# Depthwise convolution: two of three channel blocks on TensorE in four column tiles, with shifted copies fetched by way of HBM

## The chip, the cores and the metric

The kernel runs on one core of a Trainium2 chip. The metric is the device time of one execution in microseconds (us), the median of several runs. Engines are named as the profile names them: PE is TensorE (PEld its weight loads), DVE is VectorE, ACT is ScalarE, POOL is GpSimd, and SP is SyncE, which here only issues weight loads.

## The reference, cut to what matters

The reference is a stack of three transformer blocks on 256 positions of width 1024, all in fp32: one block with attention and a gated MLP, then two layers that mix the sequence and end in an MLP (dense in the first layer, a mixture of eight experts in the second). Each of the two layers has, among its mixers, a convolution module over 384 channels:

```
h = val * jax.nn.sigmoid(gate)
h = lax.conv_general_dilated(h, w_dw[:, None, :], window_strides=(1,), padding=((30, 0),),
                             feature_group_count=384) + b_dw      # 31 taps, each channel by itself
h = jax.nn.silu(layer_norm(h, ln_g, ln_b))
return h @ w_pw + b_pw
```

The depthwise convolution is 31 multiply-adds for each of 384 x 256 outputs: out[c, t] is the sum over k of w[k, c] * h[c, t - 30 + k]. The layer norm after it runs over the channels.

## The kernel before, in words

Activations of the convolution lie with channels on partitions: `hc[128, 3, 288]` holds three blocks u = 0, 1, 2 of 128 channels, with 32 zero columns ahead of the 256 positions, and `co[128, 3, 256]` takes the convolved blocks.

All weights come as slabs of 1 MB or less, in an order fixed in `plan`. SP loads a slab into a ring of buffers. ACT rounds it to its high part (`splitH`, L1461), DVE subtracts to get the low part (`splitL`, L2159), and PE multiplies three times (high by high, high by low, low by high: L567, L568, L569). ACT and DVE run some slabs ahead of PE (`hi_to`, `lo_to`, `take`). Each engine runs its own instruction stream in program order, and semaphores tie the streams together.

The convolution is inside `mixers(l)`, which is run for the layers l = 0 and 1. The slabs there are, in order: mc (three, for value and gate of blocks 1, 2, 0), mv, mv, mu, mu, ma, mo0, mo1, mo2, mo3.

- DVE's `glu` writes a finished block into `hc` (L2636), in the order 1, 2, 0.
- Blocks 1 and 2 are convolved on DVE, one instruction of 128 x 256 for each tap (L2612 for tap 0, L2615 for the others, which add to `co`). The generator `taps()` gives first three taps of block 1 and then taps of the two blocks in turn, so that two instructions after each other mostly add to different blocks. Each tap waits for the tap before it of its own block. `some_taps(n)` puts n of them between the slab splits: 3, 5, 6, 5, 5, 5, 5, 6, 9 and the 13 that are left. Of these 62, 49 lie ahead of the `catL` writes.
- Block 0 is convolved on PE: for each of the 31 taps one fp32 matmul with a diagonal 128 x 128 matrix as weights and a shifted window of `hc` as moving operand (L1027). The profile shows each fp32 matmul as two passes. POOL builds the 31 diagonal matrices (`diag`, L3119) beforehand, and then zeroes a corner of `wsT`.
- In PE's order these matmuls stand after the pooling mixer (L1005 and L1007, two column tiles of 64), and the spatial gating (L1018), and ahead of the five `cat` units: two by L1037, then three transposes of `yg` (L596). The third transpose uses the bank of the first `cat` unit again and so waits until DVE has written `catL` of that unit (L2169 in DVE's order, after nine taps).
- ACT takes block 0 out of PSUM (L1878), then writes `catH`. After `cat` come the slabs mo0 to mo3 (L567 to L569), with the layer norm's sums between them: L1061 needs all three blocks of `co`.

`catH` and `catL` lie in the buffers RBH and RBL, and so did `diag`.

Of the kernel before, what the change touches and what calls it, by code (L numbers as in the profile page):

```python
# [14 lines left out]
CAP = 128  # L15
# [27 lines left out]
def shape_constants(cap):  # L43
# [43 lines left out]
    "in_x0 in_x1 in_cb in_prm0 in_half in_rope in_prm in_mem in_mask in_grow in_band in_layer in_rt "  # L87
    "out_main out_over zero dwdiag "
# [63 lines left out]
def program(nc, x, mem, consts, w, out, cap):  # L152
    ctx = ExitStack()
    with ctx:
# [21 lines left out]
        diag = at("diag", [128, 31, 128], b0 + 64 * KB)  # L176
# [10 lines left out]
        ph = b0 + 4 * KB  # L187
        ident, ones = cb[:, 0:128], cb[:, 128:256]
# [50 lines left out]
        hc = at("hc", [128, 3, 288], ph + 35 * KB)  # L239
# [314 lines left out]
        def tensor(e):  # L554
# [406 lines left out]
            def mixers(l):  # L961
# [25 lines left out]
                t.wait_ge(S.in_layer, 80 * (l + 1))  # L987
# [10 lines left out]
                for m in range(2):  # L998
                    b = bank["pool", l, m] = ring.take()
                    t.wait_ge(S.mrow, 6 * l + 6)  # L1000
                    t.wait_ge(S.in_band, 16)
# [9 lines left out]
                for tb in range(2):  # L1011
                    b = bank["gm", l, tb] = ring.take()
                    t.wait_ge(S.ws, 2 * l + 2)
                    t.wait_ge(S.dwdiag, 32 * l + 32)
# [7 lines left out]
                b = bank["dw", l] = ring.take()  # L1022
                t.wait_ge(S.dwdiag, 32 * l + 31)
                t.wait_ge(S.th, 3 * l + 3)
                o = claim(b, (S.co0, l + 1))
                for k in range(31):
                    mm = e.matmul(o[:, 0:256], diag[:, k, :], hc[:, 0, 2 + k:258 + k], start=(k == 0), stop=(k == 30))  # L1027
                mm.then_inc(S.dw, 1)

                ring.go(range(4, 8))  # L1030
                for m in range(2):
                    b = bank["cat", l, m] = ring.take()
                    t.wait_ge(S.py, 2 * l + m + 1)
                    t.wait_ge(S.in_layer, 80 * (l + 1))
# [16 lines left out]
                for tb in range(2):  # L1051
# [3 lines left out]
                    if tb == 0:  # L1055
                        b = bank["colsum", l] = ring.take()
                        t.wait_ge(S.taps, 62 * (l + 1))
                        t.wait_ge(S.co0, l + 1)
# [392 lines left out]
        def scalar(e):  # L1451
# [287 lines left out]
            def ffn(f):  # L1739
# [42 lines left out]
                for i in range(12):  # L1782
                    G, V = fb[i % 2], fb[2 + i % 2]
                    if i == 3:
                        if f == 0:
# [3 lines left out]
                            load(band[:, :, :].rearrange("p g t -> p (g t)"), consts[:, c0:c0 + width], S.in_band)  # L1789
                            layer_loads(0)  # L1790
                        else:
# [3 lines left out]
                            a.wait_ge(S.in_grow, 16)  # L1795
# [31 lines left out]
            def mixers(l):  # L1827
# [7 lines left out]

                hi_to(mc[0] + 1)
# [297 lines left out]
        def vector(e):  # L2134
# [274 lines left out]
            def gained(i):  # L2409
                tb, o = i // 2, slice(512 * (i % 2), 512 * (i % 2) + 512)  # L2410
                v.wait_ge(S.xadd, 12)
                v.wait_ge(S.in_grow, 16)
                e.tensor_tensor(xg[:, tb, o], X[:, tb, o], grow[:, o], ALU.mult).then_inc(S.gx, 1)
# [181 lines left out]
            def mixers(l):  # L2595
# [3 lines left out]
                tapped = [62 * l]  # L2599

                def taps():

                    at = {}
                    order = [(k, 1) for k in range(3)]
                    order += [(k - 3 * (u == 2), u) for k in range(3, 34) for u in (1, 2)]
                    for k, u in order:
                        if k < 31:
                            o, src = co[:, u, :], hc[:, u, 2 + k:258 + k]
                            wk = prm[:, dwc + u + 3 * k:dwc + u + 3 * k + 1]
                            if k == 0:  # L2610
                                v.wait_ge(S.th, 3 * l + u)
                                ins = e.tensor_scalar(o, src, wk, pcol("conv_dw_b_2", 3 * l + u), ALU.mult, ALU.add)  # L2612
                            else:
                                v.wait_ge(S.taps, at[u])
                                ins = e.scalar_tensor_tensor(o, src, wk, o, ALU.mult, ALU.add)  # L2615
                            ins.then_inc(S.taps, 1)
                            tapped[0] += 1
                            at[u] = tapped[0]
                            yield
# [650 lines left out]
```

## Time and profile before

| what | value |
|---|---|
| median of 3 runs | 1807.03 us (1806.54 to 1807.79) |
| the profiled execution, its own time | 1805.34 us |
| its span in the profile | 1803.5 us |
| mean granted PE clock | 0.998 of 2.4 GHz |
| PE busy | 1734.2 us, 96% of the span |
| DVE busy | 1183.6 us, 66% |
| ACT busy | 913.9 us, 51% |
| POOL busy | 55.9 us, 3% |

The profile is of one execution, which took 1.7 us less than the median; 1.8 us of that execution's time lie outside the span. The convolution of layer 0 lies between 513 and 571 us, that of layer 1 between 796 and 854 us. The shares of busy time are averages over the whole program. What a change in one stretch is worth has to be read from that stretch.

### The profile page before, as it was taken

Reading aid. Unit: us, or ns where it says so; the run is one execution under the profiler, and the core shown is the slowest. Engines: PE = TensorE matmul, PEld = TensorE weight load, DVE = VectorE, ACT = ScalarE, POOL = GpSimd, SP = SyncE. Lnnn points to the kernel's source line nnn. Section 1 sums busy time; section 2 is a strip of 40 time slices with the busy share of each in tenths; the row PEclk is TensorE's granted clock in tenths of the full one; section 3 lists DMA queues with packets and bytes.
Section 4 is the critical chain, followed back from the end, with each engine's and each line's share of the span. In section 5 each row is a group of like instructions: output and inputs, shape, how many; then the busy total and the mean of one; then the engine's idle time right before and its main releaser. Section 6 shows DMA issues by size and latency. Waiting matters only on the chain.

```text
span 1803.5 us, 25131 instructions
## 1 busy us (share of the span) xinstructions
PE 1734.2 (96%) x10391; PEld 1421.9 (79%) x10391; DVE 1183.6 (66%) x1517; ACT 913.9 (51%) x992; POOL 55.9 (3%) x71
## 2 busy tenths in 40 slices
PE   7999998999999999999999999999999999999997
PEld 7988887899897999998777777776776777676774
DVE  6664576866788665579677665665665665765653
ACT  5445655554464444344556553555455555454542
POOL 0000000000060000050000000000000000000000
PEclk9999999999999999999999999999999999999999
DMA  9433443565544465645659999999999999999995
GB/s 322 157 94 122 151 148 113 176 233 187 170 158 140 138 219 176 209 125 203 233 210 360 370 402 383 418 412 400 364 386 383 404 385 409 410 386 400 404 410 210
DMA packets 157545, 495.13 MB, mean 275 GB/s; under 512 B 9609, under 2 KB 99439, under 8 KB 114415
## 3 DMA queue, kind: packets, MB, share of 16 engines
q1 hardware_dynamic: 152911, 489.04, 71.6%
q10 hardware_dynamic: 4512, 4.40, 0.9%
q8 instruction: 84, 1.38, 0.3%
q14 instruction: 38, 0.31, 0.0%
HBM read 492.36 MB, written 1.05 MB: 274 GB/s over the span
## 4 chain that ended last, share of the span: by engine, by line
PE 81%; DVE 11%; ACT 6%; issue 2%; DMA 0%; ACTq 0%; DVEq 0%
PE bank L567 22%; PE bank L569 21%; PE bank L568 21%; DVE splitL L2159 6%; PE bank L1233 4%; PE bank L1266 4%; ACT splitH L1461 4%; PE bank L1212 1%; DVE co L2615 1%; PE bank L1168 1%; PE bank L1027 1%; PE bank L596 1%; PE bank L710 1%; PE bank L733 1%; PE bank L1085 0%
## 5 line engine op out<-in xcount | busy, mean ns | idle before, releaser
L2159 DVE TENSOR_TENSOR splitL<-raw,splitH 128x2048 fp32r<-128x2048 f32 (+1 forms) x248 | 561.5, 2272 | 155.3 <-ACT splitH L1461 154.5
L1461 ACT ACTIVATE splitH<-raw 128x2048 fp32r<-128x2048 f32 (+2 forms) x250 | 469.5, 1889 | 118.5 <-PE bank L569 106.8
L567 PE MATMUL bank<-RAH,splitH 128*128 128x256 f32 x1088 | 311.7, 286 | 7.1 <-DVE RAL L2169 3.3
L569 PE MATMUL bank<-RAH,splitL 128*128 128x256 f32 x1088 | 307.7, 283 | 0.0
L568 PE MATMUL bank<-RAL,splitH 128*128 128x256 f32 x1088 | 307.7, 283 | 0.0
L567 PE MATMUL bank<-splitH,RBH 128*128 128x512 f32 x736 | 293.4, 399 | 3.3 <-DVE splitL L2159 3.3
L569 PE MATMUL bank<-splitH,RBL 128*128 128x512 f32 x736 | 287.5, 391 | 0.0
L568 PE MATMUL bank<-splitL,RBH 128*128 128x512 f32 x736 | 286.9, 390 | 0.0
L2159 DVE TENSOR_TENSOR splitL<-rawx,splitH 128x2048 fp32r<-128x2048 f32 x89 | 203.1, 2288 | 28.6 <-ACT splitH L1461 28.1
L567 PEld LDWEIGHTS bank<-RAH,splitH 128*128 128x128 f32 x1088 | 208.4, 192 | 11.8 <-DVE RAL L2169 4.5
L568 PEld LDWEIGHTS bank<-RAL,splitH 128*128 128x128 f32 x1088 | 208.5, 192 | 1.0
L569 PEld LDWEIGHTS bank<-RAH,splitL 128*128 128x128 f32 x1088 | 208.5, 192 | 0.0
L1461 ACT ACTIVATE splitH<-rawx 128x2048 fp32r<-128x2048 f32 x89 | 169.6, 1913 | 64.8 <-PE bank L569 64.5
L567 PEld LDWEIGHTS bank<-splitH,RBH 128*128 128x128 f32 x736 | 138.5, 188 | 39.5 <-DVE splitL L2159 10.6
L569 PEld LDWEIGHTS bank<-splitH,RBL 128*128 128x128 f32 x736 | 138.2, 188 | 29.9
L568 PEld LDWEIGHTS bank<-splitL,RBH 128*128 128x128 f32 x736 | 138.5, 188 | 26.4
L567 PE MATMUL bank<-splitH,hTH 128*128 128x512 f32 x280 | 112.9, 403 | 24.1 <-DVE splitL L2159 24.1
L1461 ACT ACTIVATE hTH<-bank 128x512 fp32r<-128x512 f32 x35 | 21.0, 599 | 204.7 <-PE bank L1212 204.7
L2877 DVE TENSOR_TENSOR hTL<-bank,hTH 128x512 fp32r<-128x512 f32 x35 | 24.1, 688 | 135.4 <-ACT hTH L1461 135.4
L568 PE MATMUL bank<-splitL,hTH 128*128 128x512 f32 x280 | 109.4, 391 | 0.0
L569 PE MATMUL bank<-splitH,hTL 128*128 128x512 f32 x280 | 109.1, 390 | 0.0
L1233 PE MATMUL bank<-raw,xgS 128*64 128x256 f32 x864 | 100.5, 383 | 0.0
(340 smaller groups left out, 2217.7 us busy)
## 6 DMA issues: line engine op xcount, KB each, us to landing
raw<-in_moe_wg SPq DMA_DIRECT2D x71, 1024.0 KB, 7.5
raw<-in_moe_wd SPq DMA_DIRECT2D x69, 1024.0 KB, 8.7
raw<-in_moe_wu SPq DMA_DIRECT2D x68, 1024.0 KB, 9.0
rawx<-in_moe_wu SPq DMA_DIRECT2D x44, 1024.0 KB, 8.5
rawx<-in_moe_wd SPq DMA_DIRECT2D x43, 1024.0 KB, 9.0
rawx<-in_moe_wg SPq DMA_DIRECT2D x41, 1024.0 KB, 9.4
raw<-in_w_in SPq DMA_DIRECT2D x24, 1024.0 KB, 6.5
raw<-in_w_up SPq DMA_DIRECT2D x22, 1024.0 KB, 5.1
```

Source lines behind the costliest of these rows:

```text
L567: e.matmul(o, lh, rh, start=start, stop=False)
L568: e.matmul(o, lh, rl, start=False, stop=False)
L569: return e.matmul(o, ll, rh, start=False, stop=stop)
L596: mm = e.transpose(o[:, tb * 128:tb * 128 + 128], src[:, tb, k * 128:(k + 1) * 128], ident)
L710: mm = e.matmul(o[c][:, x0:x0 + wide], qA[p0:p0 + 64, h // 2, tb * 128:tb * 128 + 128], kA[p0:p0 + 64, h // 2, 0:wide], start=True, stop=True)
L733: mm = e.matmul(o[(j % 2) * 64:(j % 2) * 64 + 64, tb * 128:tb * 128 + 128], vA[:, sb, h * 64:(h + 1) * 64], PT[q % 2][:, x0 * 128:(x0 + 1) ...
L1027: mm = e.matmul(o[:, 0:256], diag[:, k, :], hc[:, 0, 2 + k:258 + k], start=(k == 0), stop=(k == 30))
L1233: mm = e.matmul(o[64 * h:64 * h + 64, 0:256], xgS[:, kk, 64 * (j - 5):64 * (j - 4)], V[:, k, 256 * h:256 * h + 256], start=kk == 0, stop=k ...
L1266: mm = e.matmul(banks[2][64 * half:64 * half + 64, :], hTS[q % 2][:, 128 * k + 64 * s:128 * k + 64 * s + 64], V[:, k, 512 * half:512 * hal ...
L1461: return e.activation(o, src, ACT.Copy)
L2159: e.tensor_tensor(l[:, 0:size], raws[home[n]][:, 0:size], h[:, 0:size].bitcast(F), ALU.subtract)\
L2877: e.tensor_tensor(hTL[q % 2][:, :], banks[bank["h", q]][:, :], hTH[q % 2][:, :].bitcast(F), ALU.subtract).then_inc(S.ht_lo, 1)
```

## The change

Block 0 and block 2 are now both convolved on PE, and DVE keeps block 1 alone.

For a PE block, four taps are stacked on the 128 rows of the array: partition 32 j + c of a new tile `hs` holds channel c of a group of 32 channels, shifted by j positions. There are four groups of 32 channels (i), each with its own 32 columns of the array, so that its output lands on partitions 32 i to 32 i + 31 of one bank. Eight matmuls (g) cover 32 taps, the last one with zero weights. The weights (`stack`, eight 128 x 32 matrices for each i and each of two blocks, 1 MB for a layer) are laid out on the host and loaded by ACT's queue at the start of `mixers(l)`.

The shifted copies can't be made within a partition, so POOL's queue writes the block from SBUF to HBM and then reads it back four times, each time one position further, into 32 partitions of `hs`. It waits for the write before it issues the reads, and for the reads before it goes on to the next block. Block 2 comes first, then block 0. The diagonal matrices and their building on POOL are gone. The order of `some_taps` calls is as before, but the generator now has 31 taps, each of which waits for the one right before it.

```diff
+        stack = at("stack", [128, 2, 4, 8, 32], b0 + 64 * KB)
+        hs = [at("hs2", [128, 4, 288], b0 + 72 * KB)]
...
+        hs.append(at("hs0", [128, 4, 288], ph + 42 * KB))
...
-                b = bank["dw", l] = ring.take()
-                t.wait_ge(S.dwdiag, 32 * l + 31)
-                t.wait_ge(S.th, 3 * l + 3)
-                o = claim(b, (S.co0, l + 1))
-                for k in range(31):
-                    mm = e.matmul(o[:, 0:256], diag[:, k, :], hc[:, 0, 2 + k:258 + k], start=(k == 0), stop=(k == 30))
-                mm.then_inc(S.dw, 1)
+                t.wait_ge(S.in_layer, 96 * (l + 1))
+                for v in range(2):
+                    b = bank["dw", l, v] = ring.take()
+                    t.wait_ge(S.hs, 160 * l + 80 * v + 80)
+                    o = claim(b, (S.co0, 2 * l + v + 1))
+                    for g in range(8):
+                        for i in range(4):
+                            mm = e.matmul(o[32 * i:32 * i + 32, 0:256], stack[:, v, i, g, :],
+                                          hs[v][:, i, 2 + 4 * g:258 + 4 * g], start=(g == 0), stop=(g == 7))
+                    mm.then_inc(S.dw, 1)
...
+                load(stack[:, :, :, :, :].rearrange("p v i g c -> p (v i g c)"), stacks[l], S.in_layer)
                 hi_to(mc[0] + 1)
...
-                a.wait_ge(S.dw, l + 1)
-                e.activation(co[:, 0, :], banks[bank["dw", l]][:, 0:256], ACT.Identity,
-                             bias=pcol("conv_dw_b_2", 3 * l)).then_inc(S.co0, 1)
+                for v in range(2):
+                    a.wait_ge(S.dw, 2 * l + v + 1)
+                    e.activation(co[:, 2 - 2 * v, :], banks[bank["dw", l, v]][:, 0:256], ACT.Identity,
+                                 bias=pcol("conv_dw_b_2", 3 * l + 2 - 2 * v)).then_inc(S.co0, 1)
...
-                    order = [(k, 1) for k in range(3)]
-                    order += [(k - 3 * (u == 2), u) for k in range(3, 34) for u in (1, 2)]
-                    for k, u in order:
...
+                    o = co[:, 1, :]
+                    for k in range(31):
+                        src = hc[:, 1, 2 + k:258 + k]
+                        wk = prm[:, dwc + 1 + 3 * k:dwc + 1 + 3 * k + 1]
...
+                            v.wait_ge(S.taps, tapped[0])
+                            ins = e.scalar_tensor_tensor(o, src, wk, o, ALU.mult, ALU.add)
...
+            def shifted(l, v, u):
+                g.wait_ge(S.th, 3 * l + v + 2)
+                e.dma_start(turned_out[l, v], hc[:, u, :]).then_inc(S.hs, 16)
+                g.wait_ge(S.hs, 160 * l + 80 * v + 16)
+                for j in range(4):
+                    e.dma_start(hs[v][32 * j:32 * j + 32, :, :],
+                                turned_out[l, v][:, j:j + 288].rearrange("(i c) x -> c i x", i=4)).then_inc(S.hs, 16)
+                g.wait_ge(S.hs, 160 * l + 80 * v + 80)
...
             for l in range(2):
-                dwc = PCOL["conv_dw_w_2"] + 93 * l
-                g.wait_ge(S.xadd, 12 + 8 * l)
-                for k in range(31):
-                    e.tensor_scalar(diag[:, k, :], ident, prm[:, dwc + 3 * k:dwc + 3 * k + 1], None, ALU.mult)\
-                        .then_inc(S.dwdiag, 1)
-                g.wait_ge(S.ws_turn, l + 1)
-                g.wait_ge(S.dwdiag, 32 * l + 31)
-                e.memset(wsT[64:128, :, 0:64], 0.0).then_inc(S.dwdiag, 1)
+                for v, u in enumerate((2, 0)):
+                    shifted(l, v, u)
```

Waits follow from this: PE and DVE wait for six loads of a layer in place of five (`in_layer`), L1061's sums wait for 31 taps and both PE blocks, DVE's `dd` waits for both too, since `hs` of block 0 lies where `dd` is written, and the zeroing of `wsT` is done once, early.

## Rows read from the trace of the kernel before

**Rows 1.** Stretches: busy us of PE, PEld, DVE, ACT, POOL; then PEclk, DMA share, GB/s.

```profile
511.00:562.00 51.00, 49.93 (x323) 46.30 (x322) 48.76 (x111) 26.93 (x40) 18.11 (x19) 1.00 0.58 190
794.00:845.00 51.00, 50.44 (x330) 47.15 (x329) 46.92 (x98) 25.02 (x37) 16.82 (x19) 1.00 0.59 200
```

**Rows 2.** PE's waits from 510 to 570 us: total, times, longest.

```profile
PE bank L596 <- DVE RBL L2169: 0.5, 1, 0.5
PE bank L567 <- DVE splitL L2159: 0.3, 1, 0.3
```

**Rows 3.** PE's timeline in layer 0: start, us, instruction, [idle before <- releaser].

```profile
546.62 13.58 PE L1027 MATMUL bank<-hc,diag 128*128 128x256 f32 x62
560.13 1.08 PE L1037 MATMUL bank<-py,plw 64*64 64x256 f32 x8
...
562.33 0.44 PE L596 MATMUL bank<-cb,yg 128*128 128x128 f32 x2 [0.54 <-DVE RBL L2169]
```

**Rows 4.** PE's timeline in layer 1.

```profile
829.84 13.58 PE L1027 MATMUL bank<-hc,diag 128*128 128x256 f32 x62
843.35 1.08 PE L1037 MATMUL bank<-py,plw 64*64 64x256 f32 x8
```

**Rows 5.** DVE's timeline in layer 0.

```profile
516.39 1.00 DVE L2615 SCALAR_TENSOR_TENSOR co<-hc,prm,co 128x256 f32<-128x256 f32 x2
...
518.68 0.42 DVE L2636 TENSOR_TENSOR hc<-bank,sgc 128x256 f32<-128x256 f32 x1
...
528.36 0.42 DVE L2636 TENSOR_TENSOR hc<-bank,sgc 128x256 f32<-128x256 f32 x1
...
531.92 2.06 DVE L2615 SCALAR_TENSOR_TENSOR co<-hc,prm,co 128x256 f32<-128x256 f32 x5
...
554.24 1.88 DVE L2676 SCALAR_TENSOR_TENSOR yg<-bank,prm,uu 128x96 f32<-128x96 f32 x8
...
558.24 3.64 DVE L2615 SCALAR_TENSOR_TENSOR co<-hc,prm,co 128x256 f32<-128x256 f32 x9
561.80 0.87 DVE L2169 SCALAR_TENSOR_TENSOR RBL<-bank,prm,RBH 128x256 fp32r<-128x256 f32 x2
```

**Rows 6.** DVE's timeline in layer 1.

```profile
801.72 0.42 DVE L2636 TENSOR_TENSOR hc<-bank,sgc 128x256 f32<-128x256 f32 x1
...
840.32 3.65 DVE L2615 SCALAR_TENSOR_TENSOR co<-hc,prm,co 128x256 f32<-128x256 f32 x9
844.56 0.92 DVE L2169 SCALAR_TENSOR_TENSOR RBL<-bank,prm,RBH 128x256 fp32r<-128x256 f32 x2 [0.60 <-ACT RBH L1497]
```

**Rows 7.** Costliest groups, two column tiles of 64, all of the run: busy us, mean ns.

```profile
L1233 PE MATMUL bank<-raw,xgS 128*64 128x256 f32 x864 | 100.5, 383 | 0.0
```

**Rows 8.** PE's timeline in layer 0, two column tiles of 64.

```profile
543.25 0.66 PE L1005 MATMUL bank<-band,at_rows 128*64 128x256 f32 x4 [0.56 <-ACT at_rows L1861]
543.74 0.40 PE L1007 MATMUL bank<-band,at_rows 128*64 128x128 f32 x4
543.95 0.65 PE L1005 MATMUL bank<-band,at_rows 128*64 128x256 f32 x4
```

**Rows 9.** Groups of instructions, 510 to 600 us: passes of two columns.

```profile
L1068 PE MATMUL bank<-cb,sq 128*128 128x2 f32 x12 | 1.5, 253 | 0.2 <-ACT sq L1891 0.2
```

**Rows 10.** DMA issues: count, KB each, median us from issue to landing.

```profile
out<-Z SPq DMA_DIRECT2D x2, 512.0 KB, 3.2
...
c<-in_shape_constants ACTq DMA_DIRECT2D x1, 164.0 KB, 12.0
cb<-in_shape_constants ACTq DMA_DIRECT2D x1, 128.0 KB, 4.3
```

**Rows 11.** Busy time by stretch: mixers' start, and the experts.

```profile
500.00:510.00 10.00, 9.34 (x76) 8.90 (x75) 8.23 (x36) 8.15 (x17) 9.62 (x14) 1.00 0.02 8
...
1000.00:1700.00 700.00, 679.24 (x3538) 493.23 (x3537) 446.61 (x303) 364.73 (x288) 0.00 (x0) 1.00 0.98 395
```

**Rows 12.** PE's waits from 1000 to 1700 us, all of them.

```profile
PE bank L567 <- DVE splitL L2159: 20.8, 18, 1.2
```

More of the change, by code:

```diff
@@ L149, in halves, with program @@
     return (0, 2, 1, 3).index(tb_half) + 1
-def program(nc, x, mem, consts, w, out, cap):
+def program(nc, x, mem, consts, stacks, w, out, cap):
     ctx = ExitStack()
@@ L1056, in mixers @@
                         b = bank["colsum", l] = ring.take()
-                        t.wait_ge(S.taps, 62 * (l + 1))
-                        t.wait_ge(S.co0, l + 1)
+                        t.wait_ge(S.taps, 31 * (l + 1))
+                        t.wait_ge(S.co0, 2 * l + 2)
                         o = claim(b, (S.dd, 6 * l + 3))
@@ L1788, in ffn @@
                             c0, width = CCOL["band"]
-                            load(band[:, :, :].rearrange("p g t -> p (g t)"), consts[:, c0:c0 + width], S.in_band)
+                            load(band[:, :, :].rearrange("p g t -> p (g t)"), consts[:, c0:c0 + width], S.in_grow)
                             layer_loads(0)
@@ L2598, in mixers @@
                 dwc = PCOL["conv_dw_w_2"] + 93 * l
-                tapped = [62 * l]
+                tapped = [31 * l]
                 def taps():
-                    at = {}
-                    order = [(k, 1) for k in range(3)]
-                    order += [(k - 3 * (u == 2), u) for k in range(3, 34) for u in (1, 2)]
-                    for k, u in order:
[L2607 to L2619, printed above, removed]
+                    o = co[:, 1, :]
+                    for k in range(31):
+                        src = hc[:, 1, 2 + k:258 + k]
+                        wk = prm[:, dwc + 1 + 3 * k:dwc + 1 + 3 * k + 1]
+                        if k == 0:
+                            v.wait_ge(S.th, 3 * l + 1)
+                            ins = e.tensor_scalar(o, src, wk, pcol("conv_dw_b_2", 3 * l + 1), ALU.mult, ALU.add)
+                        else:
+                            v.wait_ge(S.taps, tapped[0])
+                            ins = e.scalar_tensor_tensor(o, src, wk, o, ALU.mult, ALU.add)
+                        ins.then_inc(S.taps, 1)
+                        tapped[0] += 1
+                        yield
                 more = taps()
@@ L3250, in by_slabs, with tap_stacks @@
     return np.ascontiguousarray(m.reshape(8, 2, 4, 128, 7, 512).transpose(0, 4, 1, 3, 2, 5)).reshape(8, 7, 2, 128, 2048)
+def tap_stacks(taps):
+    rows = np.zeros((2, 32, 384), np.float32)
+    rows[:, 0:31] = taps
+    rows = rows.reshape(2, 8, 4, 3, 4, 32).transpose(0, 2, 5, 3, 4, 1)[:, :, :, [2, 0]]
+    stacks = np.zeros((2, 4, 32, 2, 4, 8, 32), np.float32)
+    for c in range(32):
+        stacks[:, :, c, :, :, :, c] = rows[:, :, c]
+    return stacks.reshape(2, 128, 2048)
 def kernel(**inputs):
@@ L3266 @@
     out = nc.dram_tensor("out_0", (1, 256, 1024), F, kind="ExternalOutput").ap()
-    program(nc, aps["x"], aps["mem"], aps["shape_constants"], {n: aps[n] for n in WEIGHTS}, out, CAP)
+    program(nc, aps["x"], aps["mem"], aps["shape_constants"], aps["stacks"], {n: aps[n] for n in WEIGHTS}, out, CAP)
     r = run_bass_kernel_spmd(nc, [feeds], core_ids=[0])
```

33 lines of the change are left out of this document (20 added, 13 removed).

## The prediction

> **What bounds the kernel now.** I read the busy time by stretch first. In both stretches of the convolution PE is busy for all but about 1 us of 51, at a granted clock of 1.00, and DVE for all but 2 to 4 us [rows 1]. So neither share alone names the bound: each may be late for the other. PE's waits say who is late: in layer 0 it waits for DVE twice, 0.3 us for a slab's low part and 0.5 us for `catL` [rows 2]. PE is the bound by a hair, and DVE stands right behind it. The timelines then give the place where the two meet in both layers: the third transpose of `yg` (L596), which can't start before DVE has written `catL` of the first `cat` unit. I call its start the meeting point. In layer 0 it is at 562.33, 0.53 us after DVE began that write at 561.80, and PE had waited 0.54 us [rows 3, 5]. In layer 1 DVE was done with its taps at 840.32 + 3.65 = 843.97, waited 0.60 us for ACT and began the write at 844.56 [rows 6], so the meeting point is 844.56 + 0.53 = 845.09. ACT's way from PE's first `cat` matmul to that write is 844.56 - 843.35 = 1.21 us [rows 4, 6]; the way from PE's last convolution matmul to the meeting point is thus 1.21 + 0.53 = 1.74 us when DVE isn't late. Behind it PE runs slabs that were split long before, so what the meeting point gains, the end gains.
>
> **PE's convolution.** Removed: 31 matmuls, 62 passes, 13.58 us in each layer [rows 3, 4], 0.219 us a pass. Added: 2 blocks x 8 x 4 matmuls = 64, 128 passes of as many columns (256). The trace has no four column tiles of 32. It has two of 64: 864 passes took 100.5 us, 0.116 each [rows 7], against 0.219 for the full array, so two tiles run side by side. Bounds: from 128 / 4 x 0.219 = 7.0 us, if four do too, to 128 x 0.116 = 14.9 us, if four do no better than two. Weight loads don't stand against the lower one: passes of two columns, which cost little but their load of 128 columns, took 1.5 / 12 = 0.125 us [rows 9]; a quarter of that, four times, is 0.125 in a period of 0.219. Nor does the rate of instructions, as far as the trace goes: eight passes with their loads started in 543.95 - 543.25 = 0.70 us, 0.088 each [rows 8], which the array itself set; four tiles need 0.055. I take 7.0: what limits two tiles there is the streaming of columns, and each tile has its own.
>
> The Trainium skill's page TensorE: Matmul & The Clock Gate (Part 3, measured speedup) gives 2.38x for three column tiles; at that efficiency four would give 3.2x and the convolution would take 28.0 / 3.2 = 8.8 us, an estimate. The same page's Part 1 has about 62 ns of sequencer time per matmul where hardware decoding is off: 128 of them make 7.9 us. The rows here show neither for four tiles.
>
> **DVE's taps.** Two blocks in turn: nine taps less five take 3.64 - 2.06 = 1.58 us, 0.395 each; the last of five then lasts 2.06 - 4 x 0.395 = 0.48. Two taps of one block, the second waiting for the first, take 1.00, so they start 0.52 apart [rows 5]. The new generator has only such taps. Of the 49 taps ahead of the meeting point the first three stay as they are. The other 46 cost 46 x 0.395 = 18.2 us; the 28 that replace them come in groups of 5, 6, 5, 5, 5, 2, and cost 22 x 0.52 + 6 x 0.395 = 13.8 us. DVE reaches its `catL` write 4.4 us earlier, not the 7.1 that 18 taps fewer would give. All 31 are done before L1061's sums, and the 13 late ones go from a place where PE didn't wait for them: 0.
>
> There is also a loss. The groups of 5 and 6 lie ahead of the last mu slab's split, with 9 starts 0.125 us later each: 1.1 us. In layer 0 PE already waited 0.3 for that split [rows 2], so PE is 1.1 us later from there on, and starts the convolution at 546.62 + 1.1 = 547.7. In layer 1 no such wait is on the list, and I take 0.
>
> The skill's page VectorE: DVE Perf Modes (The DRAIN you can't avoid) says that a semaphore between two instructions costs nothing extra. These rows show 0.125 us for it, and go before the rule; what it would make of the sum is a rival below.
>
> **The sum.** Layer 0: by PE the meeting point comes at 547.7 + 7.0 + 1.74 = 556.4, by DVE at 562.33 - 4.4 = 557.9. The later one holds: 4.4 us. Layer 1: by PE 829.84 + 7.0 + 1.74 = 838.6, by DVE 843.97 - 4.4 + 0.53 = 840.1, against 845.09: 5.0 us. Together 9.4. So DVE becomes the bound at this point, and PE's convolution may take up to 557.9 - 1.74 - 547.7 = 8.5 us in layer 0 and 8.5 in layer 1 at no cost. Above that each us costs one in each layer.
>
> **The transfers.** Block 2 is in `hc` at 518.68 + 0.42 = 519.1, block 0 at 528.8 [rows 5]. PE wants block 2 at 547.7 and block 0 3.5 us later, at 551.2. POOL does one trip after the other: a write of 150 KB, its landing, four reads of about 147 KB, their landing. POOL issues no DMA in this trace. Nearest rows, issue to landing: 3.2 us for a write, 4.3 for 128 KB, 12.0 for 164 KB behind other loads [rows 10]. A trip is between 3.2 + 4.3 = 7.5 and 24 us. I take 10, nearer to the low rows, since the DMA engines are busy 0.58 of the time here [rows 1]; it ends at 529 and 539, long before. PE never waits up to a trip of (551.2 - 519.1) / 2 = 16.0 us, in layer 1 (833.3 - 802.1) / 2 = 15.6 [rows 4, 6]; with DVE's lateness as a further cover the meeting point stays up to (557.9 - 1.74 - 3.5 - 519.1) / 2 = 16.8 and 16.4. Beyond it nobody but PE is held, but behind PE stand the `cat` units and all the rest.
>
> **At nothing.** ACT issues the load of `stack`, 1 MB, as the mixers begin, in a stretch (500 to 510) where the DMA engines are busy 0.02 of the time [rows 11]; PE first asks for the layer's loads behind the last mu slab, which it can't start before DVE's taps at 531.92 [rows 5]. Block 2's way out of PSUM runs on ACT while PE convolves block 0. The diagonal matrices: nobody waited for POOL at the convolution; if POOL slowed DVE, its going gives at most some tenths, and I count 0. From `cat` on, the experts' stage included, the gain is carried on: from 1000 to 1700 the DMA engines are busy 0.98 of the time [rows 11], but PE waits 20.8 us of 700 in all, and none of it for a DMA [rows 12].
>
> The profiled execution took 1805.34 us, 1.8 more than its span; less 9.4 that is 1795.9. The median of the runs stands 1.7 us above it, so 1807.03 - 9.4 = 1797.6. This kernel's runs tell a change from none at about 0.2%, 3.6 us.
>
> **Rivals.**
>
> A. *Three tiles' worth*: the four tiles overlap only in part. At 28.0 / 3 = 9.3 us the cover of 8.5 is passed by 0.8 in each layer: 1799.2; at 11 us, 1802.6. Nothing in the trace speaks for it but that nothing shows more than two.
>
> B. *Pairs only*: 14.9 us. Layer 0: 547.7 + 14.9 + 1.74 = 564.3, 2.0 late; layer 1: 846.5, 1.4 late: 1810.4, no change that can be told. It loses its point if passes of one tile show starts 0.22 apart.
>
> C. *Transfers late*, the one on the other side: the trip is longer than 16.8 us. Each us more comes twice, once for each block, in each layer, 4 us in all: the gain of 9.4 is gone at 18.9 us a trip, and it is slower by over 0.2% from 19.8. At 24: block 0 lands at 567.1, the meeting point is at 567.1 + 3.5 + 1.74 = 572.3, 10.0 late, in layer 1 10.3 late: 1827. For it: a busy queue did take 12.0 a step. Against: that was behind a row of others. The skill's page SBUF - State Buffer (SBUF: two separate sides) adds that POOL builds its DMAs' descriptors itself and is locked out of SBUF while DVE runs in a two-port mode: 3.1 in place of 0.62 us in its example. Two steps of 2.5 us more would still leave the trip of 10 at 15, an estimate; no run here shows it.
>
> D. *Taps cheaper than read*: a tap that waits costs no more than one that doesn't, as by the page on VectorE. DVE gains 7.1 us, and PE sets the meeting point: layer 0 at 546.62 + 7.0 + 1.74 = 555.4, 6.9 earlier, layer 1 6.5 earlier: 1793.6. The row of 1.00 us speaks against it.
>
> E. *Swallowed by the experts' stage*: its loads bound it, and layer 1's 5.0 us are lost: 1802.6.
>
> **Chances.** The forecast 0.59, A 0.12, B 0.09, C 0.11, D 0.06, E 0.03. Faster are the forecast, A, D and E: 0.80. Within 0.2%: B but for its edge and a little of C, 0.09. Slower: the rest, 0.11. The range leaves out B and C, 0.20, and takes in D at the low end and A and E at the high: 1793 to 1805.
>
> **What the new profile would show.** L1027's successor in about 7 us a layer, two blocks of 3.5, the tiles' passes starting in fours; DVE's taps 0.52 apart, its `catL` write at about 557.4 and 839.6; PE waiting about 1.5 us for DVE at the meeting point and 1.4 at the last mu split of layer 0; POOL's trips of about 10 us, ended before PE asks. A wait of PE at the first convolution matmul would show C, passes at 0.11 us B. The prediction is wrong if DVE, now the bound, has a wait in its chain that I took as its own work.

## The result, and the profile after

| | before | after |
|---|---|---|
| median of the runs (four each) | 1806.78 us | 1795.63 us |
| ratio of the two, 95% interval | | 0.9942 (0.9930 to 0.9954) |
| the profiled execution, its span | 1803.5 us | 1794.3 us |
| PE, DVE, ACT, POOL busy | 1734.2, 1183.6, 913.9, 55.9 us | 1723.7, 1160.2, 914.4, 12.5 us |

The ratio is 10.5 us faster (8.3 to 12.6); the medians stand 11.1 apart, the spans 9.2. Forecast were 9.4 us and 1797.6.

The stretches up to the meeting points, columns as in [rows 1]:

```profile
511.00:558.00 47.00, 44.76 (x399) 39.84 (x397) 43.98 (x92) 27.95 (x41) 5.62 (x10) 1.00 0.71 216
785.00:836.00 51.00, 49.42 (x441) 44.95 (x440) 46.14 (x101) 29.07 (x42) 5.48 (x10) 1.00 0.67 206
```

DVE is busy for all but 3 us of 47, though it lost half its taps, and PE has 2.2 us idle where it had 1.1: both have less to do, and neither was left far ahead. PE's waits in layer 0, from 505 to 570 us (total, times, longest), where [rows 2] had 0.5 and 0.3:

```profile
PE bank L599 <- DVE RBL L2177: 1.1, 1, 1.1
PE bank L570 <- DVE splitL L2167: 1.0, 1, 1.0
PE bank L1008 <- ACT at_rows L1868: 0.8, 1, 0.8
```

PE's timeline in both layers (start, us, instruction, [idle before <- releaser]), which answers to [rows 3, 4]. L1032 is the convolution, L599 the transposes, L570 a slab's high by high pass, L1008 the pooling:

```profile
533.82 0.45 PE L570 MATMUL bank<-splitH,RAH 128*128 128x384 f32 x1 [0.98 <-DVE splitL L2167]
...
545.33 0.66 PE L1008 MATMUL bank<-band,at_rows 128*64 128x256 f32 x4 [0.76 <-ACT at_rows L1868]
...
548.79 7.12 PE L1032 MATMUL bank<-hs,stack 128*32 128x256 f32 x128
...
558.58 0.44 PE L599 MATMUL bank<-cb,yg 128*128 128x128 f32 x2 [1.08 <-DVE RBL L2177]
...
826.18 7.12 PE L1032 MATMUL bank<-hs,stack 128*32 128x256 f32 x128
...
835.91 0.44 PE L599 MATMUL bank<-cb,yg 128*128 128x128 f32 x2 [1.02 <-DVE RBL L2177]
```

L1032 takes 7.12 us where the diagonal matrices took 13.58 [rows 3, 4]. The meeting point, the last L599 row of each layer, moved from 562.33 to 558.58 and from 845.09 to 835.91, and PE waits there 1.08 and 1.02 us for DVE. DVE's timeline in layer 0, as [rows 5]:

```profile
516.88 0.41 DVE L2617 TENSOR_SCALAR co<-hc,prm 128x256 f32<-128x256 f32 x1
...
519.94 2.56 DVE L2620 SCALAR_TENSOR_TENSOR co<-hc,prm,co 128x256 f32<-128x256 f32 x5
...
525.76 3.08 DVE L2620 SCALAR_TENSOR_TENSOR co<-hc,prm,co 128x256 f32<-128x256 f32 x6
...
532.01 1.75 DVE L2167 TENSOR_TENSOR splitL<-raw,splitH 128x1536 fp32r<-128x1536 f32 x1
...
550.93 1.00 DVE L2620 SCALAR_TENSOR_TENSOR co<-hc,prm,co 128x256 f32<-128x256 f32 x2
...
555.85 2.28 DVE L2167 TENSOR_TENSOR splitL<-raw,splitH 128x2048 fp32r<-128x2048 f32 x1
558.05 0.87 DVE L2177 SCALAR_TENSOR_TENSOR RBL<-bank,prm,RBH 128x256 fp32r<-128x256 f32 x2
```

Five taps take 2.56 us and six 3.08, each 0.52 more than one less. The split that PE waited for starts at 532.01. Ahead of `catL` (L2177) stands one more split, 2.28 us long, of a slab (mo3) that PE needs much later.

The first tap of this execution is at 516.88, that of before at 515.90, ahead of all of the change's work. Measured from the first tap, the meeting point of layer 0 is 4.7 us earlier (41.70 in place of 46.43) and that of layer 1 5.4 (first taps at 795.17 and 798.93: 40.74 in place of 46.16). So a better measure than the span is the stretch that holds all that the change touches: from the first tap of layer 0 to the layer norm's sums of layer 1 (L1067, 843.02; L1061, 852.23 before). It takes 326.14 us in place of 336.33, 10.2 less, close to the 10.5 of the ratio. Behind it both kernels take 951.3 us.

### The profile page after: what moved, and what is told of

Same layout as the page of the kernel before. It is cut to its first block, busy times and chain, and to the rows that moved or that the text cites. A ratio compares the mean times of both kernels' runs of the same rounds, so it can differ in the third digit from the quotient of the medians.

```text
span 1794.3 us, 25298 instructions
## 1 busy us (share of the span) xinstructions
PE 1723.7 (96%) x10523; PEld 1409.2 (79%) x10523; DVE 1160.2 (65%) x1455; ACT 914.4 (51%) x994; POOL 12.5 (1%) x29
## 4 chain that ended last, share of the span: by engine, by line
PE 79%; DVE 13%; ACT 6%; issue 2%; DMA 0%; ACTq 0%; DVEq 0%
PE bank L570 21%; PE bank L572 21%; PE bank L571 21%; DVE splitL L2167 7%; PE bank L1239 4%; ACT splitH L1467 4%; PE bank L1272 4%; DVE co L2620 2%; PE bank L1218 1%; PE bank L1174 1%; PE bank L599 1%; PE bank L713 1%; PE bank L736 1%; PE bank L1091 0%; DVE fb L2502 0%
## 5 line engine op out<-in xcount | busy, mean ns | idle before, releaser
L570 PE MATMUL bank<-RAH,splitH 128*128 128x256 f32 x1088 | 312.4, 287 | 6.2 <-DVE RAL L2177 3.3
L570 PE MATMUL bank<-splitH,RBH 128*128 128x512 f32 x736 | 293.9, 399 | 3.2 <-DVE splitL L2167 3.2
L570 PEld LDWEIGHTS bank<-RAH,splitH 128*128 128x128 f32 x1088 | 209.4, 192 | 10.6 <-DVE RAL L2177 4.5
L570 PEld LDWEIGHTS bank<-splitH,RBH 128*128 128x128 f32 x736 | 138.7, 189 | 39.5 <-DVE splitL L2167 10.5
L570 PE MATMUL bank<-splitH,hTH 128*128 128x512 f32 x280 | 112.8, 403 | 24.1 <-DVE splitL L2167 24.1
```

What stands on the lines that cost most here:

```text
L570: e.matmul(o, lh, rh, start=start, stop=False)
```

## The experiments

All times are compared with the kernel before on the same chip. A ratio has an interval of some 0.0012 to each side, 2.2 us, so smaller differences rest on the traces. The table has the stretch from the first tap of layer 0 to the sums of layer 1, worked out from each profile as above. Ahead of it and behind it lies the same work in every kernel, and its length scatters: the first tap lies at 515.3 to 517.0 us, the rest takes 951.0 to 951.7 us in nine of the profiles and 952.7 to 953.2 in five, whatever the kernel. The granted clock tells those profiles apart. The four with their first tap at 516.9 us (after, after_again, two_sums, tile_by_tile) have 3.4 us at half clock (1.2 GHz) from about 498 us on, and the five with the longer rest have such a stretch that begins between 874 and 889 us; the others have neither. Just ahead of the one near 498 us PE had waited 1.92 us for DVE, in the kernel before as well, where the clock stayed at 1.00, so what makes it fall in one execution and not in the other stays open. Here is that stretch in the kernel after (columns as in [rows 1]):

```profile
497.80:501.10 3.30, 3.30 (x12) 2.72 (x10) 2.00 (x5) 1.90 (x6) 0.00 (x0) 0.50 0.60 217
```

taps_in_line has such a stretch inside the measured one as well, of which more below.

| kernel | median, us | ratio (95%) | stretch, us | against after |
|---|---|---|---|---|
| before | 1806.78 | | 336.33 | +10.2 |
| after | 1795.63 | 0.9942 (0.9930 to 0.9954) | 326.14 | |
| after_again | 1796.46 | 0.9945 (0.9931 to 0.9959) | 327.07 | +0.9 |
| tiles_alone | 1807.41 | 1.0009 (1.0000 to 1.0018) | 338.13 | +12.0 |
| taps_alone | 1809.15 | 1.0016 (1.0007 to 1.0025) | 338.07 | +11.9 |
| split_late | 1794.26 | 0.9934 (0.9920 to 0.9948) | 324.04 | -2.1 |
| two_sums | 1792.47 | 0.9923 (0.9909 to 0.9937) | 322.63 | -3.5 |
| taps_in_line | 1798.38 | 0.9961 (0.9947 to 0.9975) | 328.23 | +2.1 |
| seven_late | 1791.39 | 0.9924 (0.9910 to 0.9938) | 322.57 | -3.6 |
| block_more | 1801.38 | 0.9974 (0.9963 to 0.9985) | 332.18 | +6.0 |
| tile_by_tile | 1823.99 | 1.0096 (1.0080 to 1.0111) | 354.05 | +27.9 |
| write_twice | 1800.11 | 0.9960 (0.9946 to 0.9973) | 333.51 | +7.4 |
| trip_twice | 1840.21 | 1.0189 (1.0173 to 1.0205) | 370.52 | +44.4 |
| conv_early | 1789.92 | 0.9919 (0.9905 to 0.9933) | 321.59 | -4.5 |

> The kernel after once more, unchanged, beside the three others. All theories: about 11 us under the kernel before, as in its first runs; DVE's taps 0.52 us apart, PE's waits at the meeting points 1.0 to 1.1 us.

It came as expected, but for the wait at layer 0's meeting point, of which more below.

### Each part alone

**tiles_alone**: block 0 in four tiles, DVE with both other blocks.

```diff
-                for v in range(2):
+                for v in (1,):
                     b = bank["dw", l, v] = ring.take()
...
+                    order = [(k, 1) for k in range(3)]
+                    order += [(k - 3 * (u == 2), u) for k in range(3, 34) for u in (1, 2)]
```

> From the kernel after; PE convolves block 0 alone in four column tiles, DVE has the taps of blocks 1 and 2 again, two blocks in turn as before (the load of stack and both trips stay; complete computation). My theory, that PE and DVE were both at their limit at the meeting point: PE's convolution takes 3.56 us in place of 13.58 in each layer, but the catL write still comes where DVE's 49 taps end, as before: nothing gained in layer 0, 0.6 us in layer 1, where DVE no longer waits for ACT. About 0.6 us under the kernel before, no change that can be told, and PE waits some 9 us for DVE at the meeting point. Rival, that PE's shorter convolution alone gave the gain: 2 x 10.0 = 20 us faster, or at least as fast as the kernel after (11 us under before).

Measured: no faster than before, the stretch 1.8 us longer. PE's timeline in layer 0:

```profile
546.26 3.66 PE L1032 MATMUL bank<-hs,stack 128*32 128x256 f32 x64
...
555.74 1.12 PE L599 MATMUL bank<-cb,yg 128*128 128x128 f32 x4 [4.80 <-DVE yg L2684]
561.89 0.69 PE L599 MATMUL bank<-cb,yg 128*128 128x128 f32 x2 [5.04 <-DVE RBL L2177]
```

PE was done with its convolution 10 us sooner and waited all of it away, 4.80 us for `yg` and 5.04 for `catL`. The meeting point is at 561.89, 0.44 earlier. The stretch behind it shows why even that is lost (columns as in [rows 1]):

```profile
561.00:567.00 6.00, 5.11 (x16) 4.16 (x17) 5.86 (x17) 0.38 (x1) 0.00 (x0) 0.63 0.27 94
```

The granted clock is 0.63 on average in these 6 us, after the idle time, and 16 passes of PE fall in them; in the kernel before it is 1.00 from 562 to 568 us, with 26 passes. Layer 1 shows the same: 0.69 from 845 to 851 us, 19 passes for 28. The rival, that the shorter convolution alone gives the gain, falls.

**taps_alone**: the kernel before with DVE's taps of block 1 alone. It leaves out the convolution of block 2, whose place gets the values of block 0.

```diff
                     o = claim(b, (S.co0, 2 * l + 2))
...
-                e.activation(co[:, 0, :], banks[bank["dw", l]][:, 0:256], ACT.Identity,
-                             bias=pcol("conv_dw_b_2", 3 * l)).then_inc(S.co0, 1)
+                for u in (2, 0):
+                    e.activation(co[:, u, :], banks[bank["dw", l]][:, 0:256], ACT.Identity,
+                                 bias=pcol("conv_dw_b_2", 3 * l + u)).then_inc(S.co0, 1)
```

> From the kernel before; DVE has only the 31 taps of block 1, each waiting for the one before it, and PE convolves block 0 with diagonal matrices as before. Block 2 is not convolved: ACT writes PE's block 0 to its place as well. My theory: DVE is 4.4 us earlier at the catL write, but PE's 13.58 us set the meeting point: 0.46 us gained in layer 0, 1.1 lost there by the later mu split, 0 in layer 1: about 0.6 us over the kernel before, no change that can be told. Rival, that DVE's fewer taps alone gave the gain: 8.8 to 11 us faster.

Measured: no faster than before either, the stretch 1.7 us longer. DVE's timeline, then PE's:

```profile
525.33 3.38 DVE L2613 SCALAR_TENSOR_TENSOR co<-hc,prm,co 128x256 f32<-128x256 f32 x6
...
563.23 0.88 DVE L2170 SCALAR_TENSOR_TENSOR RBL<-bank,prm,RBH 128x256 fp32r<-128x256 f32 x2 [5.21 <-ACT RBH L1497]
```

```profile
548.38 13.58 PE L1027 MATMUL bank<-hc,diag 128*128 128x256 f32 x62
...
563.77 0.44 PE L596 MATMUL bank<-cb,yg 128*128 128x128 f32 x2 [0.22 <-DVE RBL L2170]
```

DVE is 5 us ahead at `catL` and waits for ACT, which waits for PE. PE starts its convolution 1.76 us later than before (1.6 measured from the first tap), since the mu split, with dependent taps ahead of it, holds it 1.5 us (0.3 before [rows 2]). So each part alone makes the kernel no faster, and both together take 10.2 us off the stretch: PE and DVE were level, and the meeting point follows the later one.

### Who is the bound at the meeting point now

**split_late**: DVE's split of mo3 moved behind the `catL` writes.

```diff
-                lo_to(n + 4)
                 some_taps(9)
...
                     split_cols(S.cat_lo, catL[:, 2 + u, :], catH[:, 2 + u, :], banks[bank["cat", l, 2 + u]][:, 0:256])
+                lo_to(n + 4)
```

> From the kernel after; DVE's split of the slab mo3 (2.28 us), which stands right ahead of the catL writes, is moved behind them (complete computation). My theory, that DVE is the bound at the meeting point by 1.08 and 1.02 us: both waits of PE go, the meeting point is then PE's last convolution pass plus 1.74 us, 1.0 us earlier in layer 0 and 0.95 in layer 1: 1.9 us under the kernel after. Rival, that the wait comes from ACT's catH and not from DVE's place in its order: no change against the kernel after. Second rival, that mo3's split is then late for PE: slower than after by up to 2.3 us a layer.

Measured: the stretch is 2.1 us shorter than after, for 1.9 expected (the ratio alone couldn't tell). Both rivals fall: the waits at the meeting points are gone, and PE waits nowhere for mo3's split. The three transposes now follow each other:

```profile
555.09 1.17 PE L599 MATMUL bank<-cb,yg 128*128 128x128 f32 x6
```

**two_sums**: odd and even taps add to two sums.

```diff
-                    o = co[:, 1, :]
+                    sums = (co[:, 1, :], sq[:, 2, :])
                     for k in range(31):
+                        o = sums[k % 2]
...
-                            v.wait_ge(S.taps, tapped[0])
+                            v.wait_ge(S.taps, at[k % 2])
...
+                    e.tensor_tensor(sums[0], sums[0], sums[1], ALU.add).then_inc(S.taps, 1)
```

> From the kernel after; DVE's taps of block 1 add in turn to two sums, so that no tap waits for the one right before it; one more instruction adds the two sums (complete computation). My theory, that a tap that waits costs 0.125 us more: taps start 0.395 apart, DVE is 22 x 0.125 = 2.75 us earlier at the catL write and 1.1 at the last mu split. PE's waits of 1.0 us at that split in layer 0 and of 1.08 and 1.02 at the meeting points all but go: 2.95 us under the kernel after. Rival, that the 0.52 us are not the dependence but the price of any tap in this place: no change against after.

Measured: the stretch is 3.5 us shorter, for 2.95. Two taps that follow each other start 0.39 us apart, so the rival falls:

```profile
519.64 0.48 DVE L2624 SCALAR_TENSOR_TENSOR sq<-hc,prm,sq 128x256 f32<-128x256 f32 x1
520.03 0.48 DVE L2624 SCALAR_TENSOR_TENSOR co<-hc,prm,co 128x256 f32<-128x256 f32 x1
```

**taps_in_line**: the same, with the wait for the tap right before.

```diff
-                            v.wait_ge(S.taps, at[k % 2])
+                            v.wait_ge(S.taps, tapped[0])
```

> As two_sums, but each tap still waits, by its semaphore, for the tap right before it, though that one adds to the other sum (complete computation). It tells apart whether 0.52 us between starts comes from reading what the last instruction wrote or from waiting for its end at all. My theory: from the wait; taps start 0.52 us apart as in the kernel after, and the time is that of the kernel after, or 0.5 us a layer over it for the one instruction more. Rival, that a semaphore between two instructions costs nothing by itself: 0.395 us apart, and the time of two_sums, about 3 us under the kernel after.

Measured: the taps are 0.52 apart, and the rival falls. The stretch is 5.6 us longer than that of two_sums, but not all of it is the taps':

```profile
518.86 0.48 DVE L2624 SCALAR_TENSOR_TENSOR co<-hc,prm,co 128x256 f32<-128x256 f32 x1
519.38 0.48 DVE L2624 SCALAR_TENSOR_TENSOR sq<-hc,prm,sq 128x256 f32<-128x256 f32 x1
```

In this execution the clock was at half speed behind the meeting point of layer 0, first here, then the same work in the kernel after:

```profile
558.30:561.70 3.40, 3.40 (x10) 2.63 (x9) 0.49 (x2) 0.02 (x1) 0.00 (x0) 0.50 0.89 297
```

```profile
558.90:562.30 3.40, 3.40 (x18) 2.78 (x17) 1.01 (x4) 0.38 (x1) 0.00 (x0) 1.00 0.87 279
```

Half of 3.4 us is 1.7 us of PE's work. Without it the stretch is about 0.4 us over the kernel after, as expected, and 3.9 over two_sums. Both kernels read and write the same data; only the semaphore that a tap waits for differs. So the 0.125 us are the price of waiting for the end of the instruction right before. PE waits 1.7 and 1.2 us at the meeting points, more than in the kernel after, which has one instruction (0.42 us) less.

**seven_late**: the taps of the kernel after, with seven of them behind `catL`.

```diff
                 glu(1, 2)
-                some_taps(5)
...
                 for n in mu:
                     take(n)
-                    some_taps(5)
+                    some_taps(5 if n == mu[0] else 0)
...
-                some_taps(6)
...
-                some_taps(9)
```

> From the kernel after; the same 31 taps, each waiting for the one before it, but seven of them stand behind the catL writes in place of none: the group of five ahead of the last mu split is left out, and the groups behind it end seven short (complete computation). My theory, that late taps lie where nobody waits for DVE: the wait at the last mu split of layer 0 (1.0 us) goes, DVE reaches the catL writes 3.6 us earlier and both waits at the meeting points go (1.08 and 1.02): about 3 us under the kernel after, as two_sums. Rival, that taps behind catL delay the layer norm's sums or the splits of mo: seven x 0.52 = 3.6 us come back in each layer, and it is up to 4 us slower than the kernel after.

Measured: the stretch is 3.6 us shorter, for 3. DVE's timeline in layer 0:

```profile
553.95 0.92 DVE L2177 SCALAR_TENSOR_TENSOR RBL<-bank,prm,RBH 128x256 fp32r<-128x256 f32 x2
...
555.77 3.60 DVE L2620 SCALAR_TENSOR_TENSOR co<-hc,prm,co 128x256 f32<-128x256 f32 x7
```

The seven taps follow at 555.77, and no wait of PE answers to them. Late taps are free, as the prediction had it.

**block_more**: PE convolves block 0 twice.

```diff
-                    for g in range(8):
...
+                    for again in range(1 + v):
+                        for g in range(8):
...
```

> From the kernel after; PE convolves block 0 twice over into the same bank (128 + 64 passes; the result is the same). This puts a price on PE's time behind the cover: the convolution takes 7.12 + 3.56 = 10.68 us in each layer, of which the 1.08 and 1.02 us that PE waited for DVE are hidden. My theory (what passes the cover costs its full length): 2 x 3.56 - 2.10 = 5.0 us over the kernel after. Rival, that DVE's lateness covers more, or the later stages take it up: less than 2 us over after. Rival, that DVE isn't the bound at all: 7.1 us over.

Measured: 6.0 us longer, for 5.0. The convolution took 10.57 us in each layer, 3.45 more; 2 x 3.45 - 2.10 = 4.8, and in layer 1 PE waited 1.8 us for `at_rows` in place of 0.6, which makes 6.0. Both waits at the meeting points are gone. What passes DVE's cover costs its full length, and both rivals fall.

### The tiles

**tile_by_tile**: the same 128 passes, all of one tile first.

```diff
-                    for g in range(8):
-                        for i in range(4):
+                    for i in range(4):
+                        for g in range(8):
```

> From the kernel after; the same 128 passes for the two blocks, but all eight matmuls of one column tile one after another, then the next tile's, in place of the four tiles in turn (complete computation). My theory, that tiles run side by side only when the passes of different tiles follow each other: passes of one tile start 0.219 us apart, the convolution takes about 128 x 0.219 = 28 us less what neighbouring tiles share, in place of 7.12: about 2 x 21 - 2.1 = 39 us over the kernel after. Rival, that PE looks far enough ahead to overlap them in any order, or that a pass of 32 columns is short in itself: no change.

Measured: 27.9 us longer. PE's timeline, and the passes of L1032 that start in two microseconds (PE busy, PEld busy, clock, DMA share, GB/s), first here, then in the kernel after:

```profile
548.93 21.99 PE L1032 MATMUL bank<-hs,stack 128*32 128x256 f32 x128
```

```profile
549.00:551.00 2.00, 2.00 (x10) 1.04 (x11) 1.00 0.84 342
```

```profile
549.00:551.00 2.00, 2.00 (x44) 1.19 (x40) 1.00 0.85 348
```

Ten passes in 2 us in place of some forty: passes of one tile start 0.22 us apart, as those of the full array do. The whole is 21.99 us and not 28, since the single records show the first passes of the next tile starting while the last three or four of the tile before still run. The loss is 2 x 14.87 - 2.10 = 27.6 us. My 39 had too little overlap in it; the rival falls.

### The transfers

**write_twice** and **trip_twice**: each block written twice before it is read, and in the second kernel also read twice over.

```diff
-                e.dma_start(turned_out[l, v], hc[:, u, :]).then_inc(S.hs, 16)
...
+                for again in range(2):
+                    e.dma_start(turned_out[l, v], hc[:, u, :]).then_inc(S.hs, 16)
+                    base += 16
+                    g.wait_ge(S.hs, base)
+                for again in range(1):
+                    for j in range(4):
...
```

In trip_twice the second `range(1)` is `range(2)`.

> From the kernel after; POOL writes each block to HBM twice, one write after the other's landing, before it reads (complete computation): a trip of 10.5 us becomes one of about 14. My theory, with a cover of about 16 us a trip before PE waits: no change against the kernel after. Rival, that PE or DVE is already held by the transfers: some 3 to 7 us a layer over after.

> From the kernel after; POOL writes each block twice and reads it back twice over (complete computation): a trip of about 21 us. Block 2 would land at 520.6 + 21 = 541.6, still before PE asks (548.8), block 0 at 562.7, when PE asked at 552.4. My theory (beyond the cover each us of trip costs two in each layer): PE waits 10.3 us at the second block, the meeting point is at 562.7 + 3.56 + 1.74 = 568.0 in place of 558.6: about 9.4 us in each layer, 19 us over the kernel after. Rival, that the trips' steps overlap or shrink when repeated and the cover holds: under 4 us over after.

Measured: 7.4 us longer and 44.4 us longer. The 7.4 is one execution of 1804.04 us, the slowest of six; the fastest took 1794.78, no longer than the kernel after, and by the ratios write_twice is 3.3 us longer. In both I was short on the price of a trip. PE's timeline in layer 0 of write_twice, and its stretches of the two blocks:

```profile
547.82 3.66 PE L1032 MATMUL bank<-hs,stack 128*32 128x256 f32 x64
556.60 5.35 PE L1032 MATMUL bank<-hs,stack 128*32 128x256 f32 x64 [5.12 <-DMA hs<-shifted]
```

```profile
547.80:551.40 3.60, 3.60 (x65) 1.96 (x64) 3.56 (x4) 2.44 (x4) 2.21 (x4) 1.00 0.93 281
556.60:561.80 5.20, 5.20 (x64) 2.66 (x64) 0.74 (x1) 0.00 (x0) 0.00 (x0) 0.67 1.10 348
```

Its trips take 18.7 us each in layer 0 (519.25 to 537.90 to 556.60) and 16.3 in layer 1. PE asks for block 0 at 551.5, so by the prediction's rule it waits 519.25 + 2 x 18.7 - 551.5 = 5.1 us, and does; in layer 1 1.67. The cover of 16 us a trip is right; that the trip grows by only 3.5 us was wrong. The second write took 3.2 to 5.0 us itself, but in layer 0 the steps around it grew as well: block 2's reads took 12.6 us for 9.2, block 0's first write 6.6 for 3.9. Then the clock: behind the idle 5.12 us the same 64 passes take 5.35 us, with a granted clock of 0.67 on average, 0.50 (1.2 GHz) in the middle of it, against 3.66 at 1.00. 5.1 of wait and 1.7 of slow clock less 1.1 in layer 0, and 1.7 less 1.0 in layer 1, make 6.4 of the 7.4 us. In trip_twice, trips take 24 to 28 us:

```profile
570.23 6.22 PE L1032 MATMUL bank<-hs,stack 128*32 128x256 f32 x64 [19.17 <-DMA hs<-shifted]
```

19.17 us of wait and 6.22 - 3.66 = 2.56 of slow clock, less 1.08 that was waited for DVE anyway, make 20.7 us in layer 0; layer 1 has 22.18 of wait, 2.09 of slow clock, less 1.02, 23.2; together 43.9. So rival C was a real danger, and dearer than I priced it: 44 us for a doubled trip, not 19. C in the prediction has 1827 for trips of 24 us, without a term for the clock; trips of 24 to 28 us gave 1840.

### A version that beats both

**conv_early**: two_sums and split_late together, and block 2 convolved ahead of the pooling (the edits of the two are as above).

```diff
+                conv(0)
                 for m in range(2):
                     b = bank["pool", l, m] = ring.take()
...
+                conv(1)
```

> two_sums and split_late together, and PE convolves block 2 ahead of the pooling matmuls in place of behind them (complete computation). DVE's two edits aim at the same waits, so that together they give no more than two_sums alone. My theory for PE's order: its wait for ACT's at_rows ahead of the pooling (0.56 us in each layer) is covered by block 2's 3.56 us: 1.1 us under two_sums, some 14.5 us under the kernel before. Rival, that block 2's passes ahead of pooling only move the wait to the spatial gating or to cat, whose inputs come later from ACT and DVE: no gain over two_sums, or up to 1 us over it.

Measured: the stretch is 4.5 us shorter than after and 1.04 shorter than two_sums, for 1.1; the median is 15.5 us under before on the same chip (14.6 by the ratio, which doesn't tell it from two_sums or seven_late). The pooling follows the convolution without a wait, and none is left at the meeting points:

```profile
541.51 3.66 PE L1008 MATMUL bank<-hs,stack 128*32 128x256 f32 x64
545.10 0.66 PE L1020 MATMUL bank<-band,at_rows 128*64 128x256 f32 x4
```

## Why the prediction was right

**PE's convolution** (taken 7.0, bounds 7.0 to 14.9): 7.12 us in both layers. Rivals A and B fall. The bound from one row of the full array and one of two tiles held, on the condition that tile_by_tile shows: neighbouring passes must go to different tiles. The estimates by the page TensorE: Matmul & The Clock Gate of the Trainium skill (Part 3, measured speedup, 8.8 us; Part 1, 62 ns a matmul, 7.9 us) were both too long for this case: 0.0556 us a pass.

**DVE's taps** (0.52 against 0.395; 4.4 us earlier at `catL`): confirmed by the rows and by two_sums against taps_in_line. Rival D falls; its price was right, since two_sums, in which taps do cost 0.395, came to 1792.47 us for 1793.6. The Trainium skill's rule in VectorE: DVE Perf Modes (The DRAIN you can't avoid), that a semaphore costs nothing extra, is measured there on a semaphore after each copy. Here every tap has one in both kernels, and it is the wait for the tap right before that costs 0.125 us.

The term was short by 0.4 us a layer, and it is one that I had set at nothing: POOL's building of the diagonal matrices. In tiles_alone, where DVE's work is that of before and POOL builds none, first tap to `catL` takes 45.50 us in place of 45.90; six taps take 2.46 in place of 2.55. In taps_alone, where POOL builds them, six dependent taps take 3.38 us in place of 3.08. Before and taps_alone show the longer taps only while POOL builds (to 528.8 and 527.6 us); the next five taps take 2.06 us in before as in tiles_alone, and 2.56 in taps_alone as in after. With it 4.4 becomes 4.8 (4.7 read) and 5.0 becomes 5.4 (5.4 read).

**DVE the bound at the meeting point, PE waiting 1.5 us**: right in kind, 1.08 and 1.02 in size. In layer 0 most of the difference is again POOL's: DVE came 4.7 us earlier in place of 4.4, and PE was 0.1 us later than forecast. split_late, two_sums and seven_late each took the wait away. The cover for PE's convolution was 8.2 and 8.1 us (7.12 and the wait) rather than 8.5.

**The mu split** (1.1 us later): PE's convolution starts 31.91 us after the first tap in place of 30.72, 1.2 later; the wait is 1.0 for 1.4. That 1.2 lies so near to 1.1 is partly luck. The split delayed PE by only 0.8 us (its first matmul of that slab starts 16.94 us after the first tap in place of 16.15), since the 0.3 from POOL came back here too; another 0.2 are a longer wait for `at_rows`, which was not in the sum.

**The transfers** (10 us, bounds 7.5 to 24; cover 16). POOL's timeline:

```profile
520.63 0.69 POOL L3120 DMA_DIRECT2D shifted<-hc  x1 [217.63 <-DVE hc L2640]
523.33 2.18 POOL L3123 DMA_DIRECT2D hs<-shifted  x4 [2.00 <-DMA shifted<-hc]
532.51 0.56 POOL L3120 DMA_DIRECT2D shifted<-hc  x1 [7.01 <-DMA hs<-shifted]
536.44 2.18 POOL L3123 DMA_DIRECT2D hs<-shifted  x4 [3.37 <-DMA shifted<-hc]
...
798.89 0.56 POOL L3120 DMA_DIRECT2D shifted<-hc  x1 [260.27 <-DVE hc L2640]
...
811.59 0.56 POOL L3120 DMA_DIRECT2D shifted<-hc  x1 [7.50 <-DMA hs<-shifted]
```

Block 2's trip takes 11.9 us in layer 0 (520.63 to 532.51) and 12.7 in layer 1, block 0's 11.1 and 14.2 by the landing of its last read (543.64 and 825.79), so 10 was too short in all four. Block 0 lands some 9 us before PE asks in layer 0, but only 3.9 in layer 1. The cover was confirmed by write_twice. What I left out is that the trips crowd others. Loads from 500 to 570 us (KB each, median us to landing), first before, then after:

```profile
raw<-in_w_out SPq DMA_DIRECT2D x4, 1024.0 KB, 5.0
...
raw<-in_w_in SPq DMA_DIRECT2D x1, 1024.0 KB, 5.4
```

```profile
raw<-in_w_out SPq DMA_DIRECT2D x4, 1024.0 KB, 7.1
...
raw<-in_w_in SPq DMA_DIRECT2D x1, 1024.0 KB, 9.2
```

The Trainium skill's page DMA: Bandwidth & Descriptors (Issuing engines are not separate DMA queues) says that transfers of all engines share the same DMA engines, and the rows agree. So do the other profiles: in the two kernels without trips (before, taps_alone) these loads land in 5.0 to 5.1 and 5.2 to 5.4 us, in the twelve with trips in 5.6 to 8.7 and 6.3 to 9.2. A slab that lands late makes ACT late, as in the second profile of the kernel after (ACT's split, then PE):

```profile
542.59 1.91 ACT L1467 ACTIVATE splitH<-raw 128x2048 fp32r<-128x2048 f32 x1 [3.12 <-DMA raw<-in_w_out]
```

```profile
547.24 0.66 PE L1008 MATMUL bank<-band,at_rows 128*64 128x256 f32 x4 [2.65 <-ACT at_rows L1868]
...
558.75 1.17 PE L599 MATMUL bank<-cb,yg 128*128 128x128 f32 x6
```

There PE waits 2.65 us for ACT's `at_rows` (0.56 before [rows 8]) and no longer for DVE at the meeting point. In that execution ACT has taken DVE's place as the bound of layer 0, and the stretch is 0.9 us longer. That the trips cause this delay is argued from the landings, not tried: no kernel has the new convolution without them.

**The experts' stage** (rival E): PE's waits over the same 700 us, which were 20.8 [rows 12]:

```profile
PE bank L570 <- DVE splitL L2167: 20.9, 19, 1.2
```

Nothing of the gain was swallowed; the rest behind the stretch is 951.3 us in both.

## What to carry to other kernels

Where two engines are both within a few per cent of the whole stretch, look for the instruction at which they meet and work out both paths to it; a part of a change alone can be worth nothing and both parts 10 us, and the gain is what the later path gives. Of the path that is then the bound, first move what nobody waits for (a split, seven taps) behind that point, and keep chained instructions from waiting for the one right before. A transfer that is hidden has a cover that can be worked out, but price its trip from busy rows, since beyond the cover it costs its delay on each trip and then PE's clock.

## What the runs showed of the hardware

- Four column tiles of 32 run side by side in fp32 at 0.0556 us a pass of 256 columns, if successive passes go to different tiles, and at 0.22 if they don't.
- After 5 us without work PE ran at half its clock for a few us more: 5.35 us for 3.66 of work, and after 19 us 6.22.
- Some executions have 3.4 us at half clock where others of the same work have none, after the same wait of 1.9 us. Each costs about 1.6 us (the part behind the stretch takes 952.7 to 953.2 us for 951.0 to 951.7), as much as some of the edits here.
- A DVE instruction that waits for the one right before starts 0.125 us later, whether or not it reads what that one wrote.
- POOL was held 2.7 to 7.1 us by the same write of 146 KB to HBM (issue and wait), and twice the steps made a trip of 11 to 14 us one of 24 to 28.
- POOL's building of the diagonal matrices, while it ran, made DVE's taps up to 10% longer (3.38 us for 3.08).
